# A layer with routed experts on one core: the routing chain written anew, with scans, moved constants and one table

## The reference, cut to what matters

```python
def hier_moe(x, grp_w, grp_b, exp_w, exp_b, w_gate, w_up, w_down):
    gl = (xt @ grp_w + grp_b).astype(jnp.float32)            # 4 groups
    pg = jax.nn.softmax(gl, axis=-1)
    g_idx = jnp.argmax(gl, axis=-1)
    pg_top = jnp.take_along_axis(pg, g_idx[:, None], axis=1)[:, 0]
    el = (xt @ exp_w + exp_b).astype(jnp.float32).reshape(T, N_GROUPS, EXPERTS_PER_GROUP)
    sel = jnp.take_along_axis(el, g_idx[:, None, None], axis=1)[:, 0]
    vals, idx = lax.top_k(sel, TOP_K_INNER)                  # 2 of 8
    w = pg_top[:, None] * jax.nn.softmax(vals, axis=-1)
    expert_id = g_idx[:, None] * EXPERTS_PER_GROUP + idx
    ...
    for e in range(N_EXPERTS):                               # 32
        h = jax.nn.silu(xt @ w_gate[e]) * (xt @ w_up[e])
        y = y + combine[:, e:e + 1] * (h @ w_down[e])
```

## Time and profile before

| | us |
|---|---|
| runs, without profile | 1683.86, 1684.97, 1691.19 (median 1684.97) |
| the profiled execution, own time | 1687.71 |
| its span | 1684.5 |
| TensorE, busy | 1506.4 (89%) |
| VectorE, busy | 942.9 (56%) |
| ScalarE, GpSimd, busy | 370.5 and 368.4 |

### The profile page before, as it was taken

The page is one execution under the profiler, slowest core; times in us unless marked ns, Lnnn a source line. Parts: engine busy times, 40 slices in busy tenths (PEclk is TensorE's granted clock), DMA queues, the critical chain, the costliest instruction groups (busy, mean ns, idle before and its releaser), DMA issues. The chain is left out here.

```text
span 1684.5 us, 22742 instructions
## 1 busy us (share of the span) xinstructions
PE 1506.4 (89%) x8546; PEld 1091.8 (65%) x8546; DVE 942.9 (56%) x1580; ACT 370.5 (22%) x710; POOL 368.4 (22%) x624
## 2 busy tenths in 40 slices
PE   6689988999996999849999988998299999999985
PEld 2467766444444788638888874554288888888852
DVE  3867875466635999975665641534623333333326
ACT  2553342011110111135755550100000000000004
POOL 0330230111110000000312237654122122122204
PEclk9799999999998999979999988999579999999998
DMA  9422113233330221130000013113249898898845
GB/s 290 169 68 82 60 57 131 89 112 108 118 116 19 82 69 57 50 110 1 2 1 2 2 48 128 63 63 123 77 171 327 325 332 333 324 337 322 302 175 222
DMA packets 102965, 230.28 MB, mean 137 GB/s; under 512 B 12807, under 2 KB 70727, under 8 KB 94120
## 3 DMA queue, kind: packets, MB, share of 16 engines
q1 hardware_dynamic: 78968, 195.86, 32.8%
q0 software_dynamic: 10960, 20.80, 3.5%
q10 hardware_dynamic: 12960, 12.59, 2.2%
HBM read 204.66 MB, written 40.01 MB: 145 GB/s over the span
## 5 line engine op out<-in xcount | busy, mean ns | idle before, releaser
L1086 PE MATMUL PS<-buffer 128*128 128x128 f32 (+8 forms) x5674 | 1263.9, 381 | 107.5 <-DVE buffer L1576 52.0
L1086 PEld LDWEIGHTS PS<-buffer 128*128 128x128 f32 (+2 forms) x5674 | 879.7, 196 | 464.0 <-issue 309.0
L1576 DVE TENSOR_TENSOR buffer<-buffer 128x256 f32<-128x256 f32 (+18 forms) x467 | 264.8, 587 | 20.2 <-ACT buffer L836 5.6
L1089 PE MATMUL PS<-buffer 128*128 128x128 f32 x1176 | 166.7, 285 | 34.0 <-DVE buffer L1576 24.6
L1089 PEld LDWEIGHTS PS<-buffer 128*128 128x128 f32 x1176 | 137.9, 156 | 63.2 <-issue 49.1
L1576 DVE TENSOR_TENSOR buffer<-PS,buffer 128x512 f32<-128x512 f32 (+3 forms) x143 | 94.0, 684 | 144.2 <-PE PS L1086 126.2
L1576 DVE TENSOR_TENSOR buffer<-buffer,PS 128x256 f32<-128x256 f32 (+3 forms) x55 | 27.5, 501 | 206.4 <-PE PS L1086 195.8
L1996 DVE TENSOR_SCALAR_CACHE_REDUCE buffer<-PS 128x1152 f32<-128x1152 f32 (+1 forms) x72 | 89.2, 1239 | 41.5 <-PE PS L1086 40.5
L979 ACT ACTIVATE buffer<-buffer 128x1152 f32<-128x1152 f32 (+1 forms) x72 | 83.7, 1163 | 103.8 <-DVE buffer L1996 103.8
L1060 ACT ACTIVATE buffer<-PS 128x256 f32<-128x256 f32 x33 | 12.7, 384 | 371.3 <-PE PS L1086 293.3
L2012 DVE COPY buffer<-PS 128x640 f32<-128x640 f32 x64 | 52.8, 825 | 60.5 <-PE PS L1089 60.5
(11 more groups left out here) (162 smaller groups left out, 930.5 us busy)
## 6 DMA issues: line engine op xcount, KB each, us to landing
buffer<-in_exp_w_gate SPq DMA_DIRECT2D x33, 1024.0 KB
buffer<-in_exp_w_up SPq DMA_DIRECT2D x33, 1024.0 KB
buffer<-in_exp_w_down SPq DMA_DIRECT2D x33, 1024.0 KB
buffer<-in_w_mod SPq DMA_DIRECT2D x24, 1024.0 KB, 7.6
filter_spectra<-buffer ACTq DMA_DIRECT2D x88, 128.0 KB, 1.7
buffer<-filter_spectra SPq DMA_DIRECT2D x44, 256.0 KB, 2.6
buffer<-in_w_in SPq DMA_DIRECT2D x9, 1024.0 KB, 5.5
buffer<-expert_outputs SPq DMA_DIRECT2D x4, 1536.0 KB, 17.1
```

The source lines that it names most:

```text
L1086: return nc.tensor.matmul(out, lhsT, rhs, start=start, stop=stop)
L1089: return nc.tensor.transpose(out, in_, ident)
L1576: return dve.tensor_tensor(out, a, b, op)
```

## The change

It rewrites the routing chain and leaves all else alone.

- **Last tile.** In `first_norm(8)` the logits of tile 6 are taken before the moments; `h2` of tile 8 is made from `resid` with mean and scale as scalars, ahead of the normalised row, and GpSimd waits for the latter (`xnorm_ready`).
- **Constants.** The constants of the slots, and two new ones (`overflow_base`, `tile_starts`), are made before the first tile's normalisation. `upper` becomes `upper - ones` there.
- **Counts.** `r_all` is stored expert by expert, tile by tile, and one scan with restarts (`tile_starts` is 0 at each expert's first tile) gives `r_upto` in the place of nine additions. The subtractions for the exponentials follow it, and the weights are made after the slots.
- **Blocks.** The number of overflow blocks is rounded with a large constant (three instructions), the ends are a scan.
- **Slots.** Both choices of all tiles go through one multiplication and one sum.
- **One table.** Token number and weight lie side by side in `slot_value`; 18 matmuls of 100 columns replace 36 of 50, and TensorE starts on the first nine when the first half of the operands is there. The control words come behind these.
- **Gather.** The first gather reads `slot_token` without a copy.

```diff
@@ first_norm, on VectorE
+                if t == NLAT:
+                    take_logits(t - 2)
                 moments(resid)
-                give(dve.tensor_scalar(xnorm, resid, bn[:, 12:13], bn[:, 14:15], ALU.subtract, ALU.mult), "xnorm_ready")
                 if t == NLAT:
...
-                    own(tt(h2, xnorm, sc2[1], ALU.mult))
-                    tt(h2, h2, sh2[1], ALU.add).then_inc(sem("h2_ready"), 1)
+                    own(dve.scalar_tensor_tensor(h2, resid, bn[:, 12:13], sc2[1], ALU.subtract, ALU.mult))
+                    dve.scalar_tensor_tensor(h2, h2, bn[:, 14:15], sh2[1], ALU.mult, ALU.add).then_inc(sem("h2_ready"), 1)
                     dve.wait_ge(sem("h2_ready"), NTILE)
+                give(dve.tensor_scalar(xnorm, resid, bn[:, 12:13], bn[:, 14:15], ALU.subtract, ALU.mult), "xnorm_ready")
@@ routing, on VectorE
-            own(dve.memset(r_before[:, 0, :], 0.0))
-            for t in range(NTILE):
-                ins = tt(r_before[:, t + 1, :], r_before[:, t, :], r_all[:, t, :], ALU.add)
-                own(ins) if t + 1 < NTILE else give(ins, "routing_ready")
+            own(tt(r_all.rearrange("p (n t) -> p t n", t=NTILE), r_mask[:, 0, :, :], r_mask[:, 1, :, :], ALU.add))
+            give(dve.tensor_tensor_scan(r_upto, tile_starts, r_all, 0.0, ALU.mult, ALU.add), "routing_ready")
...
-            own(dve.tensor_copy(r_count, bank(1, NEXP)))
-            own(dve.tensor_scalar(r_blocks, r_count, float(P), None, ALU.is_gt))
-            for m in range(2, NTILE):
-                own(dve.scalar_tensor_tensor(r_blocks, r_count, float(P * m), r_blocks, ALU.is_gt, ALU.add))
-            own(dve.tensor_copy(r_scan[:, 0, :], r_blocks))
-            for i in range(5):
-                src, dst, step = r_scan[:, i % 2, :], r_scan[:, (i + 1) % 2, :], 1 << i
-                own(dve.tensor_copy(dst[:, 0:step], src[:, 0:step]))
-                own(tt(dst[:, step:], src[:, step:], src[:, 0:NEXP - step], ALU.add))
+            own(dve.tensor_scalar(r_blocks, count, 1.0 / P, -(0.5 + 0.5 / P), ALU.mult, ALU.add))
+            own(dve.tensor_scalar(r_blocks, r_blocks, ROUND_MAGIC, None, ALU.add))
+            own(dve.tensor_scalar(r_blocks, r_blocks, -ROUND_MAGIC, 0.0, ALU.add, ALU.max))
+            own(dve.tensor_tensor_scan(r_ends, ones[:, 0:NEXP], r_blocks, 0.0, ALU.mult, ALU.add))
...
-            for c in range(2):
-                own(tt(r_mask[:, c, :, :], r_mask[:, c, :, :], r_slot, ALU.mult))
-                own(dve.tensor_reduce(r_pos[:, NTILE * c:NTILE * (c + 1)], r_mask[:, c, :, :], AX.X, ALU.add))
+            own(tt(r_slots, r_mask, r_slot.unsqueeze(1).broadcast_to([P, 2, NTILE, NEXP]), ALU.mult))
+            own(dve.tensor_reduce(r_pos, r_slots.rearrange("p c t n -> p (c t) n"), AX.X, ALU.add))
...
+            for c in range(2):
+                i0, i1 = NTILE * c, NTILE * (c + 1)
+                own(tt(r_hot[:, i0:i1, :], row128.unsqueeze(1).broadcast_to([P, NTILE, P]),
+                       r_rowblk[:, 0, i0:i1].unsqueeze(2).broadcast_to([P, NTILE, P]), ALU.is_equal))
+                own(tt(r_blk[:, i0:i1, :], row128[:, 0:MAX_BLOCKS].unsqueeze(1).broadcast_to([P, NTILE, MAX_BLOCKS]),
+                       r_rowblk[:, 1, i0:i1].unsqueeze(2).broadcast_to([P, NTILE, MAX_BLOCKS]), ALU.is_equal))
+                both = [P, NTILE, 2, MAX_BLOCKS]
+                give(tt(r_pair[:, i0:i1, :, :], r_blk[:, i0:i1, :].unsqueeze(2).broadcast_to(both),
+                        slot_value[:, c, :, :].unsqueeze(3).broadcast_to(both), ALU.mult), "routing_ready")
@@ on TensorE
-            pe.wait_ge(sem("routing_ready"), 2)
-            for i in range(2 * NTILE):
-                last = mm(bank(4, MAX_BLOCKS), r_hot[:, i, :], r_number[:, i, :], i == 0, i == 2 * NTILE - 1)
+            for c in range(2):
+                pe.wait_ge(sem("routing_ready"), 2 + c)
+                for i in range(NTILE * c, NTILE * (c + 1)):
+                    last = mm(bank(4, 2 * MAX_BLOCKS), r_hot[:, i, :], r_pair[:, i, :, :].rearrange("p s n -> p (s n)"),
+                              i == 0, i == 2 * NTILE - 1)
...
-            pe.wait_ge(sem("route_done"), 1)
+            pe.wait_ge(sem("control_ready"), 1)
```

More of the change, by code:

```diff
@@ L215, in build @@
         slot_of = keep.take(2 * NTILE).bitcast(I32)
-        mix_w = keep.take(2 * NTILE, "p (c t) -> p c t", c=2)
+        slot_value = keep.take(4 * NTILE, "p (c t s) -> p c t s", c=2, t=NTILE)
+        mix_w = slot_value[:, :, :, 1]
         bn = keep.take(48)
@@ L2051, in take_logits @@
                 give(tt(logits[:, t, :], bank(1, ROUTE_W), route_bias, ALU.add), "logits_ready")
+            own(dve.tensor_copy(control[:, 0:NEXP], row128[0:1, 0:NEXP]))
+            scaled(first_slot, row128[:, 0:NEXP], float(P))
+            own(dve.tensor_scalar(overflow_base, first_slot, -1.0, float(P * (NEXP - 1)), ALU.mult, ALU.add))
+            own(dve.tensor_scalar(no_row, row128[:, 0:MAX_BLOCKS], float(2 * T + 3 * P - NO_ROW), ident[:, P - 1:P], ALU.add, ALU.mult))
+            own(dve.tensor_scalar(no_row, no_row, float(NO_ROW + 1), None, ALU.add))
+            own(dve.tensor_scalar(no_token, ident[:, P - 1:P], float(-NO_ROW), float(NO_ROW + 1), ALU.mult, ALU.add))
+            for rows, first in ((slot_row[:, 0:1], 2 * T), (clear_row[:, 0:1], 2 * T + P), (clear_row[:, 1:2], 2 * T + 2 * P)):
+                own(dve.tensor_scalar(rows, token_no[:, 0:1], float(first - 1), None, ALU.add))
+            own(dve.tensor_copy(slot_value[:, :, :, 0], token_no[:, 0:2 * NTILE].rearrange("p (c t) -> p c t", c=2)))
+            sub(upper, upper, ones)
+            for r in range(2):
+                dve.wait_ge(sem(f"mod_stored{r}"), 16 * ((MOD_CHUNKS - COND_CHUNKS) // 2))
+            own(dve.memset(tile_starts, 1.0))
+            own(dve.memset(tile_starts.rearrange("p (n t) -> p n t", t=NTILE)[:, :, 0], 0.0))
             dve.wait_ge(sem("g1_loaded"), 32)
@@ L2103, in _ @@
-            own(dve.tensor_copy(control[:, 0:NEXP], row128[0:1, 0:NEXP]))
-            scaled(first_slot, row128[:, 0:NEXP], float(P))
-            own(dve.tensor_scalar(no_row, row128[:, 0:MAX_BLOCKS], float(2 * T + 3 * P - NO_ROW), ident[:, P - 1:P], ALU.add, ALU.mult))
-            own(dve.tensor_scalar(no_row, no_row, float(NO_ROW + 1), None, ALU.add))
-            own(dve.tensor_scalar(no_token, ident[:, P - 1:P], float(-NO_ROW), float(NO_ROW + 1), ALU.mult, ALU.add))
-            for rows, first in ((slot_row[:, 0:1], 2 * T), (clear_row[:, 0:1], 2 * T + P), (clear_row[:, 1:2], 2 * T + 2 * P)):
-                own(dve.tensor_scalar(rows, token_no[:, 0:1], float(first - 1), None, ALU.add))
@@ L2130, in _ @@
-            own(dve.tensor_scalar(r_eid[:, 60:61], ends[:, NEXP - 1:NEXP], float(NEXP), None, ALU.add))
-            own(dve.tensor_copy(control[:, 61:62], r_eid[0:1, 60:61]))
-            give(dve.tensor_scalar(control[:, 60:61], control[:, 61:62], 1, None, ALU.logical_shift_right), "control_ready")
-            scaled(upper, ident, ALPHA)
-            sub(r_base, ends, r_blocks)
-            own(dve.tensor_scalar(r_base, r_base, float(NEXP - 1), float(P), ALU.add, ALU.mult))
-            sub(r_base, r_base, first_slot)
@@ L2139, in _ @@
+            axpy(r_base, r_base, float(P), overflow_base)
+            rank = bank(0, NTILE * NEXP).rearrange("p (n t) -> p t n", t=NTILE)
             wide = [P, NTILE, NEXP]
@@ L2159, in _ @@
+            give(dve.tensor_scalar(control[:, 60:61], control[:, 61:62], 1, None, ALU.logical_shift_right), "control_ready")
             dve.wait_ge(sem("routing_product"), 2)
             number, empty, token = bank(4, MAX_BLOCKS), r_number[:, 0, :], r_number[:, 1, :]
-            own(dve.tensor_scalar(token, number, T + 0.5, -float(T), ALU.is_gt, ALU.mult))
+            next_but_one(dve.tensor_scalar(token, number, T + 0.5, -float(T), ALU.is_gt, ALU.mult))
+            next_but_one(dve.tensor_scalar(empty, number, 0.5, no_token, ALU.is_lt, ALU.mult))
@@ L2163, in _ @@
             own(dve.scalar_tensor_tensor(token, number, -1.0, token, ALU.add, ALU.add))
-            own(dve.tensor_scalar(empty, number, 0.5, no_token, ALU.is_lt, ALU.mult))
             give(tt(slot_token, token, empty, ALU.add), "route_done")
```

91 lines of the change are left out of this document (41 added, 50 removed).

## The result

The changed kernel takes 1672.83 us (median of 5 runs, 1672.14 to 1676.18), the kernel before, run again beside it, 1683.93 (median of 5). The ratio on record is 0.9913, with a 95% interval of 0.9893 to 0.9932; the two medians by themselves give 0.9934, so the whole times put the gain between 11 and 15 us. The forecast was 1672.5, or 12.5 us. That the total fits so well is partly luck, as the terms show: from the last projection to the start of the loop the profiled execution of the changed kernel is 13.8 us shorter and not 12.5, and three steps of the working were off by about 1 us each, not all in the same direction.

What follows compares the result with a forecast made beforehand. The serial routing chain ending in the first gather was taken as the bound. Gains of 15.2 us less a 2.7 us gather loss gave 12.5 us: 1675.2 us, or 1672.5 us from the median; range 1666.5 to 1678.5.

Steps and rivals of the forecast that it cites:

- (1): Last tile: taking tile 6's logits before the moments and tile 8's row straight from the residual gains 4.3 us.
- (2): Scores to counts: fewer VectorE instructions and one scan for nine additions gain 3.7 us, between 3.0 and 4.1.
- (3): Three counting matmuls: the constants made beside them were in their shade, so moving them gains 0.
- (4): Counts to slots, slots to table: gains of 6.5 us (5.5 to 7) and 0.4 us.
- rival B: TensorE partly at its high clock: 2 us off in the table's product, 1.3 us in the last tile; 1669.5 us, chance 0.13.
- (5): Table to gather: dropping GpSimd's copy of the indices gains 0.35 us, between 0 and 1.
- (6): First gather: now meets block 1's weights, a loss of 2.7 us, between a gain of 0.9 and 5 us lost.
- f: Stretch from the gather to the loop's first full block: forecast difference 0.
- Rival F: Loop: TensorE's return to the fast clock fails, slower than before, 1695 us with two slow blocks; chance 0.02.

Runs made afterwards that it cites:

- e4: Changed kernel with the last tile as before (logits of tile 6 after the normalisation, row from the normalised one): 1676.44 us, ratio 0.9906.
- e9: Changed kernel with ten constants made again while VectorE waits for the counting matmuls, not before tile 0: ratio 0.9906.
- e10: Changed kernel with GpSimd's copy of the index column ahead of the first gather put back: ratio 0.9901.
- e8: Changed kernel run again unaltered, as the measure for others on the same chip: 1675.75 us, ratio 0.9910.
- e1: Changed kernel with SyncE loading block 1's weights only after the first gather has landed: 1669.91 us, ratio 0.9872.
- e3: Kernel before, with only block 1's weights issued later, when the first table is there: 1695.76 us against 1689.79 beside it, ratio 1.0028.
- e6: Changed kernel with the comparison of block ends and the control words ahead of the slots, as in the kernel before: ratio 0.9886.
- e2: Changed kernel with block 1's weights, the ln2 vectors and GpSimd's clearing rows held back until the first gather landed: 1670.13 us, ratio 0.9875.

## Why the prediction was right

Point by point, by its steps:

(1) Last tile: -4.3 forecast, -4.20 measured, and e4 undoes exactly that. TensorE was slow in the turning and the last product (1.97 and 3.63 us), as assumed.

(2) Scores to counts: -3.7, measured -3.60. The scan was taken at 0.66 and is 0.76, which is the whole difference. The step of nine in the sum of the masks was taken at 0.2 and costs 0.21 (0.68 against 0.47 in the chain). By the Trainium skill (DVE: opcode table, instruction layouts, handler registers and perf-mode slots, section Datapath and trigger behaviour) the estimate was 0.76: this trace agrees, with 0.76 for 288 elements and 0.23 for 32.

(3) Constants: 0, and e9 shows it.

(4) Slots and table: -6.9, measured -7.98. Slots took 5.27 us (1195.02 to 1200.29) and not 5.6: the two reads with a step of nine, taken at 0.4 together, were free. The table took 11.77 and not 12.5: I had the matmuls at 8.0 us with a low clock and they took 7.11, since the clock rose in them. That was rival B's first half, worth 0.9 us here, and it is luck of this execution as much as of the change: the same instructions took up to 7.49 us in e10. The windows of the changed kernel (stretch, its length, TensorE busy, granted clock, DMA share, GB/s) show it:

```profile
1204.00:1207.00 3.00, 2.16 (x10) 0.50 0.00 0
1207.00:1209.00 2.00, 2.00 (x11) 0.50 0.00 0
1209.00:1212.00 3.00, 2.94 (x19) 0.69 0.02 5
```

(5) Table to gather: -0.35, measured -1.13, outside the range of 0 to 1 that I gave. This step failed. I read the 0.8 us between the copy and the gather as the gather's own preparation, since it stood in every row of the loop; but every such row had a copy ahead of it. e10 gives 0.88 us to the copy, and the other 0.25 us to VectorE.

(6) The gather's loss: +2.7, measured +3.7 and, in e8, +4.2. That the weights cause it is right and is shown by e1 and e3; its size was off. I had the packets begin 2.7 us after the issue and take 4.4 us beside the vectors' queue. The row that I read says only that nothing of the gather's queue had moved up to 1232 us. The first packet moved 3.93 us after the issue, and from there the gather took 3.18 us, with the vectors nearly done. From 1233.2 to 1236.4 us, in the kernel before:

```profile
q0 software_dynamic: 371, 1.05, 84.7%
q10 hardware_dynamic: 26, 0.05, 7.1%
```

In the changed kernel the two parts are 4.46 and 6.36 us. So the start moved by 0.5 us, and the term that was mis-sized is the time beside other queues: I took it from 4.4 to 6.6 us, three queues against two, and it went from 3.18 to 6.36, two full queues against almost none. While all three queues moved (the DMA view above) the profile counts their packets out evenly: 195, 198 and 196. The bytes are not even, 0.41 MB against 0.75 and 0.95, and the gather's queue had 18.7% of the engines' time beside 33.9% and 39.3%. The Trainium skill (DMA: Bandwidth & Descriptors, section Queues, rings and completion order) says that an engine goes round its queues packet by packet. The even counts agree with that, if what the profile calls a packet is what that section does, which no run here shows.

The two misses of (4) and (5), 1.9 us too little gain, and the one of (6), 1.0 us too little loss, partly cancel; f gave 0.6 us more, again by the clock: the product of block 0 took 9.34 us and not 9.97, since the clock rose 4.1 us after its start (1231.3) and before only 5.4 us after it (1245.1). Rival F (a clock that stays low in the loop) did not occur: in the window from 1260 to 1590 us the granted clock is 1.00.

```profile
1230.00:1232.00 2.00, 2.00 (x14) 2.00 (x14) 0.00 (x0) 0.00 (x0) 0.00 (x0) 0.67 0.41 166
1232.00:1234.00 2.00, 2.00 (x21) 2.00 (x20) 0.00 (x0) 0.38 (x1) 0.00 (x0) 1.00 0.04 16
...
1260.00:1590.00 330.00, 330.00 (x2294) 274.51 (x2293) 119.21 (x116) 11.11 (x29) 72.90 (x145) 1.00 0.90 326
```

Why TensorE's clock rises at one moment and not at another stays open: it rose in each of the twelve tables with 100 columns (5.95 to 7.49 us for the same 36 instructions, by when it did) and in neither of the two executions with 50 columns (before and e3, 15.60 us both, clock 0.50).

## What to carry to other kernels

When a chain is shortened that ends in a transfer, list what will now be in flight beside that transfer: here bulk loads that were first needed some 13 us after it had landed cost it 4 us, and one wait on the loads' side got them back. A step that is hidden behind other work is only free if what it releases does not collide with the critical transfer; e6 was faster with the control words on the chain. And where an engine issues in order, a wait that clears the way for one transfer may delay the next that is needed, as in e2.

## What the runs showed of the hardware that I had not expected

- A gather with 128 indices, of which 49 fetched a row of 4 KB, took 4.3 to 4.5 us with at most the clearing rows beside it, 6.84 and 7.44 with 1 MB of vectors (7.11 in the kernel before), 8.82 with 3 MB of weights, 10.2 to 11.5 with both.
- Its first packet moved 1.77 us after the issue with no other queue busy, and 3.7 to 4.8 us after it in every other run.
- VectorE's reads with a step of nine 4-byte elements cost no more than contiguous ones: 0.46 us for 128x288 from PSUM, as before. A write with that step does: 0.67 us against 0.46.
- An indirect transfer of GpSimd starts 0.28 us after another engine's signal, but 0.90 us after a copy of its own that it waits for.
